# Scaling the norm rows of six fronts one stage ahead, and moving a rotation into the context projection

## The reference

```
for l in range(2):                                     # first model: x and ctx, 256 rows each
    sh1, sc1, gt1, sh2, sc2, gt2 = split(silu(c) @ w_ada[l] + b_ada[l], 6)      # and the same of c_ctx
    h  = rms_norm(x,   g_mix[l]) * (1 + sc1)  + sh1
    hc = rms_norm(ctx, g_mix[l]) * (1 + csc1) + csh1
    qa, ka, va, fb, qc, kc, vc = mixer_inputs(h,  w_in[l], q_norm, k_norm, rope)   # heads normed and rotated
    qac, kac, ...              = mixer_inputs(hc, w_in[l], q_norm, k_norm, None)   # heads normed only
    o = concat(global_attention(qa, ka, va, kac, vac), fourier_mix(fb), window_attention(qc, kc, vc, kcc, vcc, sink))
    x = x + gt1 * (o @ w_out[l])
    x = x + gt2 * swiglu(rms_norm(x, g_ffn[l]) * (1 + sc2) + sh2, w_gate[l], w_up[l], w_down[l])
    if l == 0:                                         # the context is brought up to date in layer 0 only
        ctx = ctx + cgt1 * (oc @ w_out[l])             # oc: dense attention and fourier mix of the context
        ctx = ctx + cgt2 * swiglu(rms_norm(ctx, g_ffn[l]) * (1 + csc2) + csh2, ...)
x = rms_norm(x, g_final)
# second model: differential attention with Mamba-2, a SwiGLU FFN,
# then NSA with MLA (q, kc, vc, ksl, vsl, kwn, vwn, ... = split(h @ od_w_in)), then 8 experts, top 2
```

## Time and profile before

| | us |
|---|---|
| median of 3 runs | 2584.38 (2580.54 to 2586.71) |
| profiled execution, own time | 2575.79 |
| its span, first to last instruction | 2574.0 |
| TensorE busy | 2368.8 (92%) |
| VectorE busy | 1762.3 (68%) |
| ScalarE busy | 1328.7 (52%) |
| GpSimd busy | 184.7 (7%) |

### The profile page before, as it was taken

How to read it: one execution, slowest core, us unless ns; L and a number is a source line. 1 busy time by engine, 2 the same in 40 slices (tenths; PEclk the granted TensorE clock), 3 DMA queues, 4 the chain that set the end, 5 groups by cost and what they waited for, 6 DMA issues and landing times. The chain is left out here.

```text
span 2574.0 us, 44478 instructions
## 1 busy us (share of the span) xinstructions
PE 2368.8 (92%) x17063; PEld 2150.7 (84%) x17063; DVE 1762.3 (68%) x2851; ACT 1328.7 (52%) x2085; POOL 184.7 (7%) x168
## 2 busy tenths in 40 slices
PE   7898999889988989979799997788999999999998
PEld 5787989778977779979689986577999999999997
DVE  3555555655556565565755556548999999999997
ACT  2243434434433544443444442336877877777775
POOL 0500000000005000008100003000000000000000
PEclk9899999999999999989789997778999999999999
DMA  8524465256543054534045551026999999999995
GB/s 344 202 103 180 172 234 204 78 206 226 213 157 131 18 185 173 193 130 159 7 148 187 182 196 65 1 90 247 362 337 339 356 341 335 354 340 336 357 343 204
DMA packets 82229, 542.86 MB, mean 211 GB/s; under 512 B 9328, under 2 KB 9840, under 8 KB 33904
## 3 DMA queue, kind: packets, MB, share of 16 engines
q1 hardware_dynamic: 79184, 529.57, 55.5%
q10 hardware_dynamic: 2848, 10.55, 1.2%
HBM read 539.03 MB, written 1.05 MB: 210 GB/s over the span
## 5 line engine op out<-in xcount | busy, mean ns | idle before, releaser
L835 PE MATMUL bank<-w_hi,src_hi 128*128 128x256 f32 (+1 forms) x2320 | 667.8, 288 | 16.5 <-DVE src_lo L606 7.1
L836 PE MATMUL bank<-w_lo,src_hi 128*128 128x256 f32 (+1 forms) x2320 | 660.7, 285 | 0.0
L837 PE MATMUL bank<-w_hi,src_lo 128*128 128x256 f32 (+1 forms) x2320 | 659.8, 284 | 0.0
L3287 DVE TENSOR_TENSOR w_lo<-ring,w_hi 128x1024 fp32r<-128x1024 f32 x528 | 638.1, 1222 | 31.0 <-ACT w_hi L3215 20.9
L835 PEld LDWEIGHTS bank<-w_hi,src_hi 128*128 128x128 f32 x2320 | 445.9, 192 | 36.0 <-issue 24.8
L836 PEld LDWEIGHTS bank<-w_lo,src_hi 128*128 128x128 f32 x2320 | 446.5, 192 | 7.2
L837 PEld LDWEIGHTS bank<-w_hi,src_lo 128*128 128x128 f32 x2320 | 446.5, 192 | 0.7
L835 PE MATMUL bank<-src_hi,w_hi 128*128 128x256 f32 x1472 | 425.1, 289 | 4.3 <-DVE src_lo L606 3.6
L1178 DVE TENSOR_TENSOR w_lo<-ring,w_hi 128x1024 fp32r<-128x1024 f32 x260 | 318.1, 1223 | 152.6 <-ACT w_hi L1106 152.0
L836 PE MATMUL bank<-src_lo,w_hi 128*128 128x256 f32 x1472 | 419.3, 285 | 0.0
L837 PE MATMUL bank<-src_hi,w_lo 128*128 128x256 f32 x1472 | 419.0, 285 | 0.0
(11 more groups left out here) (436 smaller groups left out, 2779.4 us busy)
## 6 DMA issues: line engine op xcount, KB each, us to landing
ring<-in_moe SPq DMA_DIRECT2D x176, 1024.0 KB, 7.2
ring<-in_ffn SPq DMA_DIRECT2D x66, 1536.0 KB, 6.6
ring<-in_moe SPq DMA_DIRECT2D x176, 512.0 KB, 6.9
ring<-in_ffn_ev SPq DMA_DIRECT2D x22, 1536.0 KB, 6.5
oT<-in_w_ada SPq DMA_DIRECT2D x20, 1024.0 KB, 6.0
big<-in_w_ada SPq DMA_DIRECT2D x20, 1024.0 KB, 8.5
ring<-in_w_in SPq DMA_DIRECT2D x18, 1024.0 KB, 6.5
ring<-in_w_out SPq DMA_DIRECT2D x12, 1024.0 KB, 5.1
```

The lines of the kernel that those rows point to most:

```text
L835: pe.matmul(out, ah, bh, start=start and i == 0, stop=False, skip_group_check=True)
L836: pe.matmul(out, ah, bl, start=False, stop=False, skip_group_check=True)
L837: mm = pe.matmul(out, al, bh, start=False, stop=stop and i == n - 1, skip_group_check=True)
L3287: dve.tensor_tensor(wl, piece, wh.bitcast(F32), ALU.subtract).then_inc(p.w_lo[kind].sem, 1)
```

## The change

Six fronts get their scaled rows from the block before. `Ahead` is given to that block. After its chunk `at` VectorE squares both halves of the rows and makes the mean; GpSimd takes the root (at its list's start, or with `late` after `beside`); `wait` chunks later VectorE scales both halves into `xn`. The front then has no squares, root or scaling, and TensorE's wait for `xn` is already met. The six: x projection of layer 0 (made ahead in `adaln`), FFN of x and FFN of the context in layer 0, x projection of layer 1, and both context projections. To have a block between the last change of x and its FFN, layer 0 is reordered: both attentions, both output projections, both FFNs; `p.streams` and the riders' numbers follow. The rotation of x's first eight heads moves from the x projection to the head of the context projection; that of the other eight now follows the root of the context's heads. In the NSA projection the columns' chunks come in the order 0, 1, 3, 4, 2, 5, 6; the keys are squared after the third and the fourth chunk, and scaled and rotated one pair after the fifth and one after the sixth.

```diff
-def rsqrts(p, pool, widths, parts=P):
+def rsqrts(p, pool, widths, parts=P, first=0):
...
-        v = p.small[0:parts, 0:w]
+        v = p.small[0:parts, first:first + w]
...
 class Normed:
-    def __init__(self, rows, scale, bias=None, banks=(4, 5, 6, 7), final=None):
+    def __init__(self, rows, scale, bias=None, banks=(4, 5, 6, 7), final=None, ahead=False):
+        self.ahead = ahead
...
-        self.stats = 2 if final is not None else 1
+        self.stats = 0 if ahead else 2 if final is not None else 1
+
+class Ahead:
+    def __init__(self, rows, at, loads=0, wait=1, late=False):
+        self.rows, self.at, self.loads, self.wait, self.late = rows, at, loads, wait, late
+
+    def root(self, p, pool):
+        rsqrts(p, pool, [NT], first=36)
+
+    def step(self, p, chain, dve, c):
+        st = p.small[:, 36:36 + NT]
+        if c == self.at:
+            if self.loads:
+                dve.wait_ge(*p.sig("small_loaded")(0))
+            for t in range(NT):
+                chain(dve.tensor_tensor_reduce(out=p.xn[:, t, :], in0=self.rows[:, t, :], in1=self.rows[:, t, :],
+                                               scale=1.0, scalar=0.0, op0=ALU.mult, op1=ALU.add,
+                                               accum_out=st[:, t:t + 1]))
+            dve.tensor_scalar(st, st, 1.0 / D, EPS, ALU.mult, ALU.add).then_inc(p.meansq.sem, 1)
+        if c == self.at + self.wait:
+            rsqrt(p, dve, st)
+            for t in range(NT):
+                dve.tensor_scalar(p.xn[:, t, :], self.rows[:, t, :], st[:, t:t + 1], None,
+                                  ALU.mult).then_inc(p.sig("x_normed").sem, 1)
...
 # normed_dve
-    root(f.stats)
-    dve.tensor_scalar(p.xn[:, 0, :], f.rows[:, 0, :], st[:, 0:1], None, ALU.mult).then_inc(normed.sem, 1)
+    if not f.ahead:
+        root(f.stats)
+        dve.tensor_scalar(p.xn[:, 0, :], f.rows[:, 0, :], st[:, 0:1], None, ALU.mult).then_inc(normed.sem, 1)
...
 # normed_act
-    square(1)
+    if not f.ahead:
+        square(1)
...
-    act.wait_ge(p.rstd.sem, f.root0 + f.stats)
-    act.activation(p.xn[:, 1, :], f.rows[:, 1, :], ACT.Identity, scale=p.small[:, 1:2]).then_inc(normed.sem, 1)
+    if not f.ahead:
+        act.wait_ge(p.rstd.sem, f.root0 + f.stats)
+        act.activation(p.xn[:, 1, :], f.rows[:, 1, :], ACT.Identity, scale=p.small[:, 1:2]).then_inc(normed.sem, 1)
...
 # linear, block.gpsimd
             if is_norm:
                 rsqrts(p, pool, [NT] * front.stats)
+            if ahead is not None and not ahead.late:
+                ahead.root(p, pool)
             if beside is not None:
                 beside(pool, taken)
+            if ahead is not None and ahead.late:
+                ahead.root(p, pool)
...
 # x_heads1
-        rope_rows(chain, pool, src, p.con_at(CON1, "rope_c", NT), p.con_at(CON1, "rope_s", NT), junk)
...
 # x_turns1
-        rope_rows(pool_chain(p, pool), pool, heads_of(proj, 896, 8), p.con_at(CON1, "rope_c", NT),
-                  p.con_at(CON1, "rope_s", NT), p.big[:, 0:2048])
-        rsqrts(p, pool, [16 if queries else 4])
+        for a in (0, 896):
+            rope_rows(pool_chain(p, pool), pool, heads_of(proj, a, 8), p.con_at(CON1, "rope_c", NT),
+                      p.con_at(CON1, "rope_s", NT), p.big[:, 0:2048])
+            if a == 0:
+                rsqrts(p, pool, [16 if queries else 4])
...
 # block1
-    adaln(p, first_loads)
+    adaln(p, first_loads, Ahead(x, 3, len(first_loads)))
     for l in range(2):
-        linear(p, Normed(x, p.scl[:, 0, 0, :], mod(l, 0, 0)), 6, out=px, loads=second_loads if l == 0 else (),
-               beside=x_heads1(...), riders=...)
-        ctx_src = Normed(ctx, p.scl[:, 0, 1, :], mod(l, 0, 1))
+        linear(p, Normed(x, p.scl[:, 0, 0, :], mod(l, 0, 0), ahead=True), 6, out=px, loads=second_loads if l == 0 else (),
+               beside=x_heads1(...), riders=...,
+               ahead=Ahead(ctx, 3, len(second_loads) if l == 0 else 0, 2, True))
+        ctx_src = Normed(ctx, p.scl[:, 0, 1, :], mod(l, 0, 1), ahead=True)
...
         block1_attention(p, px, l, True)
-        linear(p, block1_mix(px), 4, residual=x, gate=mod(l, 2, 0), riders=riders(12, (0, 0, 2, 2)) if l == 0 else ())
-        ffn(p, Normed(x, p.scl[:, 1, 0, :], mod(l, 3, 0), banks=(0, 1, 2, 3)), x, mod(l, 5, 0),
-            loads=() if l == 0 else last_loads, riders=riders(16, range(2, 21, 2)) if l == 0 else ())
         if l == 0:
             block1_attention(p, pc, l, False)
-            linear(p, block1_mix(pc), 4, residual=ctx, gate=mod(l, 2, 1), riders=riders(26, (0, 0, 2, 2)))
-            ffn(p, Normed(ctx, p.scl[:, 1, 1, :], mod(l, 3, 1), banks=(0, 1, 2, 3)), ctx, mod(l, 5, 1),
-                riders=riders(30, range(2, 21, 2)), after=norm_scales(p, 1, (0, 1)))
+        linear(p, block1_mix(px), 4, residual=x, gate=mod(l, 2, 0), riders=riders(12, (0, 0, 2, 2)) if l == 0 else ())
+        if l == 0:
+            linear(p, block1_mix(pc), 4, residual=ctx, gate=mod(l, 2, 1), riders=riders(16, (0, 0, 2, 2)),
+                   ahead=Ahead(x, 1))
+        ffn(p, Normed(x, p.scl[:, 1, 0, :], mod(l, 3, 0), banks=(0, 1, 2, 3), ahead=l == 0), x, mod(l, 5, 0),
+            loads=() if l == 0 else last_loads, riders=riders(20, range(2, 21, 2)) if l == 0 else (),
+            ahead=Ahead(ctx, 4) if l == 0 else None)
+        if l == 0:
+            ffn(p, Normed(ctx, p.scl[:, 1, 1, :], mod(l, 3, 1), banks=(0, 1, 2, 3), ahead=True), ctx, mod(l, 5, 1),
+                riders=riders(30, range(2, 21, 2)), after=norm_scales(p, 1, (0, 1)), ahead=Ahead(x, 4))
...
+OD_ORDER = (0, 1, 3, 4, 2, 5, 6)
...
 # nsa_keys
-        if c in (3, 4):
-            square_sums(p, chain, dve, keys[c - 3], p.work[:, 0:256], st[:, 4 * (c - 3):4 * (c - 3) + 4])
+        if c in (2, 3):
+            square_sums(p, chain, dve, keys[c - 2], p.work[:, 0:256], st[:, 4 * (c - 2):4 * (c - 2) + 4])
+        if c == 3:
+            mean_squares(p, dve, st, HD)
         if c == 4:
-            mean_squares(p, dve, st, HD)
-        if c == 5:
             rsqrt(p, dve, st)
-            for w in range(2):
+        if c in (4, 5):
+            for w in (c - 4,):
                 scale_heads(chain, dve, keys[w], st[:, 4 * w:4 * w + 4])
```

More of the change, by code:

```diff
@@ L386, in spread_passed, with adaln @@
     p.sig("gate_spread").passed(2)
-def adaln(p, loads):
+def adaln(p, loads, ahead):
     nc = p.nc
@@ L462, in _ @@
                 dve.tensor_copy(part[:, c * PC:c * PC + PC], p.ps[c % 4][:, 0:PC]).then_inc(kept_v.sem, 1)
+                ahead.step(p, chain, dve, c)
+                ahead.step(p, chain, dve, c + 1)
             dve.wait_ge(*turned(1))
@@ L878, in linear @@
            out_at=None, loads=(), front_loads=(), beside=None, split=False,
-           riders=(), after=None, inline=None):
+           riders=(), after=None, inline=None, ahead=None):
     nc = p.nc
@@ L1038, in _ @@
                     inline(dve, chain, c)
+                if ahead is not None:
+                    ahead.step(p, chain, dve, c)
             if after is not None:
@@ L1059, in linear, with ffn @@
     p.end_stream()
-def ffn(p, front, residual, gate=None, loads=(), riders=(), after=None):
+def ffn(p, front, residual, gate=None, loads=(), riders=(), after=None, ahead=None):
     nc = p.nc
@@ L1097, in _ @@
         def _(pool):
-            rsqrts(p, pool, [NT])
+            rsqrts(p, pool, [NT] * front.stats)
+            if ahead is not None:
+                ahead.root(p, pool)
         @block.scalar
@@ L1184, in lo_last @@
                                   ALU.subtract).then_inc(p.w_lo[DOWN].sem, 1)
+            chain = Chain(dve, p.sig("dve_chain"))
             normed_dve(p, dve, front, lambda kind: lo(0, kind))
@@ L1213, in _ @@
                     rider_keep(p, dve, r)
-            chain = Chain(dve, p.sig("dve_chain"))
+                if ahead is not None:
+                    ahead.step(p, chain, dve, c)
             if after is not None:
@@ L1653, in mod @@
         return p.mod[:, l, 8 * kind:8 * kind + 8, r]
-    adaln(p, first_loads)
+    adaln(p, first_loads, Ahead(x, 3, len(first_loads)))
     for l in range(2):
-        linear(p, Normed(x, p.scl[:, 0, 0, :], mod(l, 0, 0)), 6, out=px, loads=second_loads if l == 0 else (),
-               beside=x_heads1(p, px, l, second_loads if l == 0 else ()), riders=riders(0, (0, 0, 2, 2, 4, 4)) if l == 0 else ())
-        ctx_src = Normed(ctx, p.scl[:, 0, 1, :], mod(l, 0, 1))
+        linear(p, Normed(x, p.scl[:, 0, 0, :], mod(l, 0, 0), ahead=True), 6, out=px, loads=second_loads if l == 0 else (),
+               beside=x_heads1(p, px, l, second_loads if l == 0 else ()), riders=riders(0, (0, 0, 2, 2, 4, 4)) if l == 0 else (),
+               ahead=Ahead(ctx, 3, len(second_loads) if l == 0 else 0, 2, True))
+        ctx_src = Normed(ctx, p.scl[:, 0, 1, :], mod(l, 0, 1), ahead=True)
         if l == 0:
@@ L3341, in odd_layer @@
     w_ukv = p.projc[:].rearrange("p t c -> p (t c)")[:, 2048:3072]
```

(9 more changed lines are left out.)

## The result

| us | before | after |
|---|---|---|
| median of the comparison | 2584.38 (2580.54 to 2587.86, 5 runs) | 2568.89 (2565.24 to 2571.56, 5 runs) |
| profiled execution, own time | 2575.79 | 2571.56 |
| its span | 2574.0 | 2569.8 |
| granted clock over the span | 0.948 | 0.945 |

The ratio is 0.994, 95% interval 0.9925 to 0.9955: 15.5 us less. The forecast was 2574.1, 10.3 less, with the right sign and inside the range. The forecast's ratio, 0.9960, lies in that interval and just outside the first one.

A forecast was written before the change was run, and what follows sets the result against it. TensorE is busy nearly everywhere, so gains lie at stage edges. Fronts -12.4, clock -1.5, scaling +3.0, B +3.85, F -1.25, order -0.5, NSA -1.5 make -10.3 us: 2574.1 us, range 2564 to 2582.

The forecast's parts named there:

- A: Front of the x projection, layer 0: 3.1 us saved, 0.9 gained by the clock, 1.5 lost to scaling at its end.
- B: Context projection, layer 0: front saves 2.05 us, second rotation costs 5.4 and its clock 1.3, 0.8 back; in all +3.85.
- C: Front of the FFN of x, layer 0: 3.1 us saved, and 0.9 us gained by a higher clock.
- D: Front of the FFN of the context, layer 0: 3.1 us saved, and 0.9 us gained by the clock.
- E: Front of the x projection, layer 1: 3.1 us saved, 1.2 lost by the clock, 1.5 by scaling at its end.
- F: Context projection, layer 1: 2.2 us back before it, front saves 2.05, second rotation at its end costs 3.0; sum -1.25.
- The front itself: In A, C, D, E the first product comes at T+4.75, T being the block's beginning: 3.1 us saved each, 12.4 together.
- rival (3): Weight and source halves set the pace, so the four fronts give 1.0 us each, not 3.1: 2582.5 us; chance 0.06.
- The clock: Around A, C, D, E: TensorE's pause shrinks from 4.7 to 1.2 us, so the clock may stay up; 1.5 us gained.
- Rival (4): The moved rows are not hidden: 4.4 us of VectorE work in each of six fronts, up to 2597.5 us; chance 0.05.
- Rival (1): The second rotation is hidden in B; TensorE loses 0.8 us instead of 6.7: 2568.2 us; chance 0.17.
- Rival (2): GpSimd keeps VectorE out for a whole rotation: context fronts gain nothing, B's middle costs 9.2 us: 2580.7 us; chance 0.15.

The follow-up runs named there:

- no_ahead: The changed kernel with all six `ahead` arguments off; order, NSA columns and moved rotation stay: 2585.95 us, ratio 1.0029 to the kernel before.
- rot_gap: The changed kernel, but in the context projection GpSimd waits for VectorE's eight low source halves, then makes both rotations, then the heads' root: 2560.46 us, ratio 0.9924.
- rot_gap_scale4: rot_gap with the context's rows scaled behind the fifth chunk's copy of the x projections instead of the last: 2555.91 us, ratio 0.9906.
- rot_alone: The kernel before with only the rotation of x's first eight heads moved into the context projection: 2586.88 us, ratio 1.0029.
- both_first: The changed kernel with both rotations back to back at the context projection's head, heads' root behind them, in both layers: 2573.27 us, ratio 0.9972.
- second comparison: The unchanged kernels before and after measured again: 2581.26 us before, 2568.81 us after, ratio 0.9957.

## Why the prediction was right, and where it was off

no_ahead against after shows the rows made ahead, block by block (from block start to block start), with the forecast's terms sorted the same way:

| us | A | B | C | D | E | F | sum |
|---|---|---|---|---|---|---|---|
| forecast | -2.5 | -2.05 | -4.0 | -4.0 | -0.4 | -2.05 | -15.0 |
| traces | -4.1 | -2.6 | -3.3 | -3.4 | -1.9 | -2.2 | -17.5 |

*The front itself* was right: the first product stands at T+4.6 in A, C, D and E, forecast 4.75, against T+7.84 to 7.87 before. With it rival (3) fell.

*The clock* was the weak part. C's products do run 0.12 apart in after, but they do so in no_ahead too, behind the full old pause of 4.7 us:

```profile
330.48 3.33 PE L699 MATMUL bank<-ident,big 128*128 128x128 f32 x16 [4.67 <-ACT big L671]
...
335.27:340.27 5.00, 4.28 (x36) 4.08 (x35) 4.19 (x9) 2.65 (x6) 0.00 (x0) 1.00 0.00 0
```

This window stands as far behind T as the earlier trace rows, where the clock was 0.61. C's clock there is 1.00 in eight of the nine profiles with the new order of layer 0 and 0.97 in the ninth; it is 0.54 to 0.61 in all four with the old one. Three of the nine have the old pause. So the step "the pause is shorter, so the clock may stay up" failed in C: the higher clock came with the new order, and C's 3.3 is the front alone. In A too the pause did not decide: the products started 0.12 apart in three of the eight profiles with the old front and in two of the five with the new one. D's products still start 0.21 apart, so its 0.9 did not come. In E, where I had put +1.2, the products stayed 0.12 apart in after; in rot_gap and rot_gap_scale4 about 20 of them ran 0.21 apart, and rot_gap's E is 2.1 us longer (46.1 against 44.1). So the loss exists, and after did not draw it. By the first pair alone A gained 7.2 us (59.97 to 52.76) against 3.3 forecast. But the same stretch of A, with the same code, took 55.8 to 61.3 us in six profiles, mean 58.2, and with the rows ahead 52.8 to 54.7 in five, mean 53.5. With transposes at T+3.5 and T+4.15 of the old blocks, that is 4.0 us: the rest of the 7.2 was draw. Where A's clock is high in both, rot_alone and after, the block is 1.9 us shorter, about what the front gives less the scaling at its end (3.25 - 1.5).

*The rows made ahead* were hidden, apart from the two ends as forecast. In the FFNs of layer 0 TensorE waits for no weight half. In E the first squaring stood beside GpSimd and took 2.58 us, the second 1.64, before a copy that was not yet due. Rival (4) was wrong.

*B.* Front and second rotation were right in mechanism: T+8.7 against 9.35 forecast for the second group; the wait at L317 3.83 and the earlier turn 1.13, together 4.96 against 5.4; then the low clock. B became 3.9 us longer (forecast +4.65 without the A part), and its stretch from first product to last 6.6, inside the 5 to 8 that were asked. Rival (1) fell with that wait. Rival (2) fell as well: the front's low halves were let in one by one. The Trainium skill (SBUF — State Buffer, "SBUF: two separate sides") has the lock last for one instruction. The traces of both_first agree: beside the rotations, from 95.5 to 109.1, each low half ends 0.3 us behind the end of one of GpSimd's operations, and the weight half 1.1 behind.

*F.* Forecast -1.25 with E's end; the two blocks gave -2.3 at E's end (rot_alone) and +1.2 in F (31.5 to 32.7), with the tail of 2.4 for 3.0.

*Order and NSA.* Forecast -2.0, measured +0.5 and +3.4 us with intervals that reach from -2 to +7. The NSA term failed not in its block (-2.3 against -1.5) but in what I left out: the next stage gave it back.

*The sum.* Rotation: forecast +6.7, measured +7.5. Rows made ahead: -15.0 against -17.5 by the traces and -18.6 to -23 by the ratios. Order and NSA: -2.0 against +0.5 to +3.4. Rotation and orders together: forecast +4.7, and no_ahead, which has just these, measured +7.5. So the near hit owes something to luck: by the traces the rows gave 2.5 us more than forecast, the rest cost 2.8 more, and the two errors cancel: -17.5 and +7.5 make -10.0. Right were the mechanisms of fronts, rotation and ends; wrong were those of C's clock term and of the NSA term. The second comparison's 11 us fit the sum; the first one's 15.5 are 5.2 more, and there the five runs of before had a median of 2584.38, against 2577.21, 2581.26 and 2581.86 in the three later comparisons. What made before's 29 runs in one comparison spread over 2574.75 to 2587.91 stays open beyond the draws named: A, the mixer, and the even FFN with the NSA projection.

## What to carry to other kernels

When work moves to another engine's idle time, ask not only whether that engine is idle, but also what the engine that shares memory access with it is doing at that moment. Here the same two rotations made stage B 8 us longer beside VectorE's critical operations than where it waited for ScalarE (63.6 against 55.7). Price a saved wait to the end of the next stage, not to the end of its block; before crediting a higher clock to a change, look at a run without it; and take the length of a stage from several executions before explaining a few microseconds of it.

## What the runs showed of the hardware that was not expected

Identical code in stretch A took 55.8 to 61.3 us from one execution to the next. A stage that began after a pause of 5.7 us instead of 8.1 was slower by 2.1 us in its later part, in ten profiles of ten, against three of three. One stretch of the second model, 1251 to 1255 us long, came in two lengths some 3.4 us apart, in kernels old and new. Behind a pause of TensorE of 4.7 us at front C the granted clock was 0.54 to 0.61 in four profiles and 1.00 in three others, whose blocks come in another order. When GpSimd and VectorE both had work queued, VectorE's 0.36 us low halves took 1.84 each on average (7.36 for four).
